# Two dense MLPs of a transformer kernel: the down product as seven block products instead of eight, with its block sums on GpSimd

## The reference, cut to what matters

```python
D_MODEL, SEQ, DEPTH, D_FF = 1024, 512, 2, 4096
...
def sqrelu_mlp(x, w_up, w_down):
    return jnp.square(jax.nn.relu(x @ w_up)) @ w_down
...
        x = layer_norm(ALPHA * x + mix, ln_gain[layer, 0], ln_bias[layer, 0])
        x = layer_norm(ALPHA * x + sqrelu_mlp(x, mlp_w_up[layer], mlp_w_down[layer]), ln_gain[layer, 1], ln_bias[layer, 1])
```

## Time and profile before

| what | value |
|---|---|
| median of three executions | 1917.28 us |
| their spread | 1913.70 to 1919.94 us |
| span of the profiled execution, first to last instruction | 1913.1 us |
| TensorE busy by the profile | 1859.2 us, 97% |
| VectorE busy | 1174.5 us, 61% |
| ScalarE busy | 773.4 us, 40% |
| GpSimd busy | 582.9 us, 30% |
| bytes read from HBM | 216.59 MB, 114 GB/s over the span |
| mean granted TensorE clock | 0.993 |

### The profile page before, as it was taken

How to read it: one execution, slowest core, us unless ns; L and a number is a source line. 1 busy time by engine, 2 the same in 40 slices (tenths; PEclk the granted TensorE clock), 3 DMA queues, 4 the chain that set the end, 5 groups by cost and what they waited for, 6 DMA issues and landing times.

```text
span 1913.1 us, 25510 instructions
## 1 busy us (share of the span) xinstructions
PE 1859.2 (97%) x9628; PEld 1519.7 (79%) x9628; DVE 1174.5 (61%) x2001; ACT 773.4 (40%) x1320; POOL 582.9 (30%) x442
## 2 busy tenths in 40 slices
PE   9999899999999999998999999999999999999997
PEld 7876568788888888866888888889887788888876
DVE  4568857742573542176775257555559788676766
ACT  4246643321332242385342133327445554434342
POOL 1234533100000010183210000115346557676740
PEclk9999999999999999999999999999999999999999
DMA  7321033643453132302255245421211323333344
GB/s 278 120 93 45 1 132 111 224 151 109 135 185 121 67 110 95 104 2 89 89 198 176 91 152 176 159 88 67 88 45 67 110 89 110 115 121 117 112 153 154
DMA packets 39392, 222.29 MB, mean 116 GB/s; under 512 B 5936, under 2 KB 6256, under 8 KB 18928
## 3 DMA queue, kind: packets, MB, share of 16 engines
q1 hardware_dynamic: 27616, 178.94, 26.2%
q0 software_dynamic: 11664, 41.80, 6.7%
HBM read 216.59 MB, written 2.10 MB: 114 GB/s over the span
## 4 chain that ended last, share of the span: by engine, by line
PE 78%; DVE 13%; DMA 3%; ACT 2%; POOL 2%; issue 2%; SPq 0%; POOLq 0%; ACTq 0%; DVEq 0%
PE G L421 35%; PE G L2674 7%; PE G L2560 5%; PE TR L2674 5%; PE OB L2674 5%; PE G L2581 4%; PE TR L421 2%; DMA KS_sb<-ada 2%; PE OB L421 2%; PE G L1717 2%; POOL weights_low L460 1%; PE TR L2560 1%; DVE weights_low L460 1%; PE OB L1717 1%; PE TR L1717 1%
## 5 line engine op out<-in xcount | busy, mean ns | idle before, releaser
L460 DVE TENSOR_TENSOR weights_low<-ring_sb,weights_high 128x1024 fp32r<-128x1024 f32 x206 | 255.8, 1246 | 377.4 <-ACT weights_high L454 377.3
L454 ACT ACTIVATE weights_high<-ring_sb 128x1024 fp32r<-128x1024 f32 (+1 forms) x308 | 316.2, 1032 | 398.6 <-PE OB L2674 131.3
L421 PE MATMUL G<-xt_high,weights_high 128*128 128x512 f32 (+1 forms) x1224 | 451.3, 369 | 2.3 <-issue 1.5
L421 PE MATMUL G<-xt_low,weights_high 128*128 128x512 f32 (+1 forms) x1224 | 449.0, 367 | 0.0
L421 PE MATMUL G<-xt_high,weights_low 128*128 128x512 f32 (+1 forms) x1224 | 448.9, 367 | 0.0
L460 POOL TENSOR_TENSOR weights_low<-ring_sb,weights_high 128x1024 fp32r<-128x1024 f32 (+2 forms) x102 | 245.5, 2418 | 306.7 <-ACT weights_high L454 306.7
L421 PEld LDWEIGHTS G<-xt_high,weights_high 128*128 128x128 f32 x1224 | 228.4, 187 | 43.1 <-issue 3.6
L421 PEld LDWEIGHTS G<-xt_high,weights_low 128*128 128x128 f32 x1224 | 228.4, 187 | 38.6
L421 PEld LDWEIGHTS G<-xt_low,weights_high 128*128 128x128 f32 x1224 | 228.4, 187 | 37.6
L2435 POOL DMA_DIRECT2D KS_sb<-ada x64 | 34.0, 531 | 472.2 <-DVE og_sb L3040 472.2
L2274 DVE SCALAR_TENSOR_TENSOR KS_sb<-G,cols_sb,KS_sb 128x441 f32<-128x441 f32 (+2 forms) x160 | 109.9, 687 | 65.1 <-ACT KS_sb L1991 65.1
(11 more groups left out here) (576 smaller groups left out, 3657.4 us busy)
## 6 DMA issues: line engine op xcount, KB each, us to landing
ring_sb<-chunks SPq DMA_DIRECT2D x155, 1024.0 KB, 4.9
KS_sb<-ada POOLq DMA_DIRECT2D x64, 512.0 KB, 4.7
wide_sb<-x_features SPq DMA_DIRECT2D x4, 512.0 KB, 9.2
X_sb<-slabs SPq DMA_DIRECT2D x1, 2048.0 KB, 13.9
ring_sb<-slabs SPq DMA_DIRECT2D x1, 2048.0 KB, 7.7
rows_sb<-ln_gain POOLq DMA_DIRECT2D x4, 512.0 KB, 5.1
rows_sb<-ln_bias POOLq DMA_DIRECT2D x4, 512.0 KB, 6.0
X_sb<-x SPq DMA_DIRECT2D x4, 512.0 KB, 8.8
```

The source lines that it names most:

```text
L421: mm = nc.tensor.matmul(out, lhsT=a, rhs=b, start=(3 * i + j == 0), stop=(3 * i + j == n - 1))
L454: nc.scalar.activation(quarter_part(weights(stage, n)[0], stage, n), quarter_part(raw_quarter(Q), stage, n), ACT.Copy).then_inc(w_hi, 1)
L460: tt_(out=quarter_part(wl, stage, n), in0=quarter_part(raw_quarter(Q), stage, n), in1=quarter_part(wh, stage, n), op=ALU.subtract).then_in ...
```

## The change

All 32 up quarters of an MLP now run first, and their squares stay in float32 in `wide`. The down product is then Strassen's algorithm in Winograd's order on 2x2 blocks: the 512 tokens in two halves (A1., A2.), the features in pairs of tiles (the two of a pair are the two block columns), the output in two halves of 512 columns. A pair of feature tiles is a unit; there are 16. For each unit seven block products are summed instead of eight, each 2 token tiles x 3 = 6 matmuls of 512 columns. PSUM holds only four such products at a time, so there are two sweeps over the units: P1, P2, P5, P3 first, then P6, P4, P7; the down weights are loaded twice. GpSimd makes the block sums in float32: four sums of 128x256 of the hidden features and one of 128x512 of the weights per unit in the first sweep, three of 128x512 of the weights in the second. ScalarE and VectorE then split the summed blocks into high and low parts: per unit two quarters of weights and two 128x512 blocks of features in the first sweep; 1024 and 512 columns of weights, 512 and 256 columns of features in the second. VectorE adds the finished products into `X` in 28 steps per MLP (16 before). The loads of gain and bias wait for the second sweep; the small inputs of the second block load during the first sweep of `mlp1`; the context's transposes are split in two.

```diff
-    st.add("mlp0", quarters=64, act=32, hidden=32, dve=16, ln=28, std=4)
+    st.add("mlp0", quarters=96, act=32, dve=28, ln=28, std=4)
...
+        def block_low(dve, stage, x, u):
+
+            dve.wait_ge(staged_h, staged_at(stage, x, u))
...
+            nc.vector.tensor_tensor(out=lo, in0=src, in1=hi, op=ALU.subtract).then_inc(staged_l, 1)
...
+            def last_units(stage):
+
+                q, w = st(stage, "quarters"), SPLIT0[stage] + SWEEP2
+                for u in range(2, UNITS):
+                    if u < 4:
+                        sp.wait_ge(quarters, q + SWEEP1 + 28)
+                    else:
+                        sp.wait_ge(w_lo, w + 2 * (u - 4) + 2)
+                    sp.dma_start(raw_unit(u), A["chunks"][w // 2 + u]).then_inc(raw_in[u % 2] if u % 4 < 2 else raw_x[u % 2], 16)
...
+                if NORMS[n] in MLPS:
+                    gp.wait_ge(quarters, st(NORMS[n], "quarters") + SWEEP2 + 6)
                 gp.dma_start(rows[:, 0, :], gain.partition_broadcast(P)).then_inc(gb_in, 16)
...
             gpsimd_low(gp, "mlp0")
-            gain_bias(1, A["ln_gain"][0, 1, :], A["ln_bias"][0, 1, :])
...
+                def first_weights(u):
+                    Q = SPLIT0[stage] + SWEEP1 + 2 * u
+                    gp.wait_ge(raw_in[(Q // 2) % 2], 16 * (Q // 4 + 1 - SPARED.get(stage, 0)))
+                    b11, b12 = raw_quarter(Q)[:, 0:512], raw_quarter(Q + 1)[:, 0:512]
+                    tt(out=b12, in0=b12, in1=b11, op=ALU.subtract).then_inc(raw_sums, 1)
...
+                    room_for(gp, stage, u)
+                    tt(out=s1, in0=a21, in1=a22, op=ALU.add).then_inc(hid_sums, 1)
+                    gp.wait_ge(staged_l, staged_at(stage, "0", u))
+                    gp.wait_ge(hid_sums, n + 1)
+                    tt(out=a21, in0=a11, in1=a21, op=ALU.subtract).then_inc(hid_sums, 1)
+                    gp.wait_ge(hid_sums, n + 2)
+                    tt(out=a11, in0=s1, in1=a11, op=ALU.subtract).then_inc(hid_sums, 1)
+                    gp.wait_ge(hid_sums, n + 3)
+                    tt(out=s4, in0=a12, in1=a11, op=ALU.subtract).then_inc(hid_sums, 1)
...
+                    unit_landed(gp, stage, u)
+                    tt(out=b12, in0=b22, in1=b12, op=ALU.subtract).then_inc(raw_sums, 1)
+                    gp.wait_ge(raw_sums, n + 1)
+                    tt(out=b11, in0=b12, in1=b11, op=ALU.add).then_inc(raw_sums, 1)
+                    gp.wait_ge(raw_sums, n + 2)
+                    tt(out=b21, in0=b11, in1=b21, op=ALU.subtract).then_inc(raw_sums, 1)
...
+                for u in range(1, UNITS):
+                    first_weights(u)
+                    hidden_sums(u)
+                    if stage == "mlp1" and u == 5:
+                        gpsimd_inputs(gp)
+                for u in range(UNITS):
+                    second_weights(u)
+                    if u == 6:
+                        gain()
...
+            def down_high(act, stage, n):
...
+                if n % 2:
+                    act.wait_ge(raw_sums, raw0 + (n - SWEEP1) // 2 + 1)
+                high_split(act, stage, n)
...
+                for u, ts in ((12, (0, 1)), (13, (0, 1)), (14, (0,)), (15, (0,)), (14, (1,)), (15, (1,))):
+                    second_ready("p6", u)
...
+                for u in (12, 15):
+                    for x in ("p4", "p7"):
...
+                tile0_turned(0)
+                for t in range(2):
+                    for u in (13, 14):
+                        for x in ("p4", "p7"):
...
+                        tile0_turned(1)
+                        tile1_turned()
```

More of the change, by code:

```diff
@@ L144, in build @@
     st.add("x_ctx", tr=4)
-    st.add("mlp1", quarters=64, act=32, hidden=32, dve=16, ln=52, std=8, norm=4)
+    st.add("mlp1", quarters=96, act=32, dve=28, ln=52, std=8, norm=4)
     st.add("x4", tr=8)
@@ L480, in n_quarters, with hid, hid_r, flat @@
         def n_quarters(stage):
-            return len(FFN) if stage == "ffn2" else sum(a + b for a, b in PARTS[stage])
+            return len(FFN)
+        def hid(c):
+            return wide[:, c, :]
+        def hid_r(c):
+            return (Hh, Hl)[c // 16][:, c % 16, :]
+        def flat(x):
+            return x.rearrange("p a b -> p (a b)")
+        def staged_rows(u, x):
+            if u == 0:
+                return rowsr[:, x, :], rowsr[:, 2 + x, :], flat(rows[:, :, :])[:, (2 + x) * S:(3 + x) * S]
+            r = 2 * (u % 4) + x
+            return XTh[:, r, :], XTl[:, r, :], ring[:, 0, r * S:(r + 1) * S]
@@ L2607, in ada_turn, with turn_context @@
                 nc.tensor.transpose(OB[0][:, P:2 * P], ogf[:, 0:P], ident).then_inc(ada_turned, 1)
[L2609 to L2613, removed]
+            def turn_context(r):
+                if r == 0:
+                    pe.wait_ge(ln_norm, st("ln_ctx", "norm") + 2)
+                    pe.wait_ge(dve_out, st("mlp1", "dve") + 16)
+                else:
+                    pe.wait_ge(tr_out, st("x_ctx", "tr") + 2)
+                for b in range(4 * r, 4 * r + 4):
@@ L3165, in layer_norm @@
                 started = LN_ORDER[stage][:TT] == EARLY
-                for op, t in LN_ORDER[stage][TT if started else 0:]:
+                for op, t in LN_ORDER[stage][TT if started else 2 if stage in MLPS else 0:]:
                     if (op, t) in hooks:
@@ L3345, in _ @@
             xt_low_tile("x1", 0, 3)
-            mlp("mlp0", ALPHA, 0, between("x2", 8, True))
+            mlp("mlp0", ALPHA, 0, lambda chain, last, low: {
+                ("ga", 0): low, ("bi", 0): lambda: chain(0), ("bi", 1): lambda: (chain(1), xt_low_tile("x2", 8, 0)), ("s0", 2): lambda: xt_low_tile("x2", 8, 1)})
             xt_low_tile("x2", 8, 2)
@@ L3368, in _ @@
             xt_low_tile("x3", 16, 3)
-            mlp("mlp1", ALPHA, 2)
+            mlp("mlp1", ALPHA, 2, lambda chain, last, low: {
+                ("ga", 0): low, ("bi", 0): lambda: chain(0), ("bi", 1): lambda: chain(1), ("s0'", 1): lambda: last(2)}, tile2_early=True)
             vector_second(dve, down_wait, layer_norm, first_half)
```

655 lines of the change are left out of this document (464 added, 191 removed), and 3 rows, old and new, of the table ADA_STEPS.

## The result

The changed kernel takes 2017.87 us (median of 4 runs, 2015.9 to 2021.19), the kernel before, on the same chip, 1915.49 us (1913.12 to 1919.94): a ratio of 1.0531, with a 95% interval of 1.0511 to 1.0551. The forecast was 2010 us, within 1932 to 2050. The profiled execution took 2019.65 us, 1.7 us more than its span. The forecast let the median stand 4.2 us above the span, as before; here the two are level (2017.87 and 2018.0). So the time rose by 102.4 us by the medians and by 104.9 us by the spans, where the forecast had 92.7.

What follows compares the result with a forecast made beforehand. The prediction took TensorE to bound the MLPs before the change, and GpSimd's and VectorE's common access to bound both sweeps after it. 1917.3 + 90 (both MLPs) + 3.7 (small loads) - 1 (`ada`) = 2010 us, range 1932 to 2050.

Steps and rivals of the forecast that it cites:

- The engines take turns: Down sweeps: GpSimd and VectorE, both reading two SBUF tensors, exclude each other and bound both sweeps; +45 us per MLP.
- The price of a turn: Down sweeps: VectorE's instructions add 2.83 and 2.08 us to GpSimd's time, making units 7.04 and 5.98 us.
- high bound: Down phases: hand-overs of 0.1 us per dependent GpSimd sum, 5 us at the change of sweeps; +61 per MLP, 2042.
- The tail: End of each down phase: the layer norm delays the last products, 17.9 us after the last low part, not 8.2.
- the gap named as a sign: End of each down phase: TensorE idles some 10 us between its last but one and last group.
- The seven loads: First sweep of `mlp1`: seven small loads in GpSimd's queue, 0.53 us each, add 3.7 us.
- The `ada` terms: Up phases: moved gain and bias loads relieve the first `ada` load, -1 us in `mlp0`; nothing in `mlp1`.
- Tiles 2 and 3: Behind each down phase: three additions where one stood delay their norms for the next stage, 2 us per MLP.
- the gain and bias loads: Second sweep, unit 6: their 1.1 us issue on GpSimd fits into the buffers' slack and costs nothing.
- Hidden: Both sweeps: loading weights a second time, 32 MB, costs nothing; a chunk lands in 4.9 us, within a unit.
- TensorE stays the bound: Rival, down sweeps: turns cost little, units 5.44 and 4.08 us; about 1900 us, 1877 with layer norm hidden; chance 0.11.
- The clock: Rival, down sweeps: TensorE's waits lower its clock to 1.2 GHz, units 9.7 and 7.3 us, about 2150 us; chance 0.03.

Runs made afterwards that it cites:

- run 1: Changed kernel with VectorE's low parts in the down phases made copies of the high parts, reading one SBUF tensor in place of two: 1916.02 us (one run).
- run 2: Changed kernel with GpSimd's sums of weight blocks cut to 8 columns in both sweeps, the hidden sums kept: 1922.23 us (one run).
- run 3: Changed kernel with all block sums of both MLPs moved from GpSimd into VectorE's queue, all computed: 1967.97 us, ratio 1.0277 to the kernel before.
- run 4: Changed kernel with the seven small loads of the second MLP's first sweep moved behind all its block sums: 2021.31 us, ratio 1.0553 to the kernel before.
- Run 9: Changed kernel with three of TensorE's `ada` sums per MLP one up product later, all computed: 2022.19 us, ratio 1.0566 to the kernel before.
- run 8: Changed kernel with the gain and bias loads issued behind GpSimd's last sums of the second sweep: 2020.65 us, ratio 1.0537 to the kernel before.
- run 6: Changed kernel with VectorE's eight additions from PSUM at the change of sweeps cut to 8 columns: 2018.32 us, ratio 1.0529 to the kernel before.

## Why the prediction was right, and where it was not

**The engines take turns: right.** Runs 1 to 3 each take one side's use of the common access away, and each time the units come down to what is left. With the turns gone no other bound stood in the way: a unit took TensorE's 5.44 us, and 4.1 to 4.4 in the second sweep. So in the sweeps the removed products are worth what the forecast said.

**The price of a turn: right within about 5%, and in the second sweep on the other engine.** First sweep: 6.89 us for 7.04. The five sums' means add up to 6.66 us, 2.45 more than alone, with 0.23 us of hand-overs that the forecast had only in its high bound. Second sweep: the forecast let GpSimd set the pace, 3.90 + 2.08. GpSimd took about 5 us per unit and waited for weights; VectorE, busy throughout, set it with 6.2 to 6.3 us. The error is small because the shared access is what counts, whichever engine is charged. Both are under the full sums of the two engines' times alone (8.05 and 6.9 us). So for the Trainium skill's statement that the blocked side waits for the whole instruction ("SBUF — State Buffer"; for two SBUF inputs it stands in the section "Summary: rules for kernel authors"), the trace agrees on the exclusion and not on that price as a sum: a first-sweep unit took 6.89 us for 8.05.

The forecast had 201.3 us from the end of the up products to the last low part ahead of the norm. In `mlp0` that is 497.2 to 697.5 us, 200.3: GpSimd's first sweep ends 3 us earlier than forecast, and the second sweep takes 2 us longer. With the tail's 2 us more, the down phase of `mlp0` comes out 0.1 us from its term (+43.4 for +43.3): that close it is by luck, since these errors cancel.

**The tail: 17.9 forecast, 19.9 measured** (697.5 to 717.4 us). Tile 1 was to be ready 14.3 us after that low part; it took 14.8. TensorE still had 54 products to do at that low part, not 36, so the gap named as a sign is 3.95 us and not some 10. Its end in the timeline after, which answers to the earlier trace rows:

```profile
708.72 1.28 DVE L3394 TENSOR_TENSOR xt_low<-TR,xt_high 128x512 fp32r<-128x512 f32 x2
708.85 2.35 POOL L489 TENSOR_TENSOR weights_low<-ring_sb,weights_high 128x1024 fp32r<-128x1024 f32 x1 [0.42 <-ACT weights_high L483]
709.92 2.37 DVE L3608 SCALAR_TENSOR_TENSOR X_sb<-X_sb,rstd_sb,rows_sb 128x1024 f32<-128x1024 f32 x1
...
712.38 0.45 PE L2722 MATMUL OB<-table_sb,X_sb 128*128 128x128 f32 x1 [3.95 <-issue]
```

VectorE's last scaling stands behind tile 0's low parts, as forecast, and takes 2.37 us in place of 1.28 beside GpSimd's low part for the next stage: a turn the forecast had left out. TensorE, after its wait, starts at the lower clock: the transposes take 1.60 us to the next product, where the first tile's took 0.80, and the six products behind them 2.06 us in place of 1.36. The wait put down to "issue" is the one for that scaling.

**The seven loads, +3.7 us: wrong** (run 4: nothing). The failed step is to have added an issue time on one engine to the sum while another engine was held up in the same place: the context's norm, which the kernel before had in its down run, hidden behind TensorE, and which the forecast did not price once that cover was gone. The norm's price is one of crowding too: in run 1, where VectorE has time to spare, norm and loads together lengthen their unit by 1.5 us. With the norm, `mlp1` came out at 45.9 us for 47.0 by luck.

**The `ada` terms, -1 us and nothing: wrong**, +3.2 and +3.4 us. The first load, on the chain before, has left it, with two others of the first up run; but four later ones have come onto it. The first of them in the chain of the up phase of `mlp0` (start, duration, what):

```profile
372.35 1.23 DVE weights_low L489
373.58 0.68 DVE og_sb L3373
374.38 0.49 issue
374.88 5.26 DMA KS_sb<-ada
380.17 0.76 DVE og_sb L3373
380.96 0.76 DVE og_sb L3373
381.77 0.43 PE OB L2825 x8
```

The load waits for VectorE's product of the piece before, which the new order puts behind a weight's low part, and TensorE's sum comes 8 us after that. The forecast priced the load that moved, not the order around the others. Run 9 shows that moving TensorE's sums doesn't help; another order on VectorE wasn't tried. The timelines point to a further cause: the last four sums of `mlp0` stood four up products apart before (513.4, 535.7, 558.1 and 580.4 us), without a wait, and stand three apart now (432.0, 449.9, 467.5, 485.8), 17.0 us of TensorE's work, while loads and products for one sum take 17.6 to 18.3 us. These waits grew by 2.2 us in `mlp0`; the other 1.0 us is not traced, and no run has the sums four apart.

**Tiles 2 and 3, +2 us: right in `mlp0`** (TensorE waits 2.5 us for tile 2 there), **too little in `mlp1`** (5.9 us in `w_in`). Its weights' high parts stand on ScalarE behind the norm's root, and TensorE waits for the low parts that GpSimd makes of them (timeline after):

```profile
1399.15 0.20 ACT L3090 ACTIVATE rstd_sb<-rstd_sb 128x1 f32<-128x1 f32 x1 [0.64 <-DVE rstd_sb L3592]
1399.26 2.94 ACT L483 ACTIVATE weights_high<-ring_sb 128x1024 fp32r<-128x1024 f32 x3
...
1400.38 5.74 POOL L489 TENSOR_TENSOR weights_low<-ring_sb,weights_high 128x1024 fp32r<-128x1024 f32 x2 [9.39 <-ACT weights_high L483]
...
1403.82 0.58 PE L448 MATMUL G<-hidden_low,weights_high 128*128 128x256 f32 x1 [5.16 <-POOL weights_low L489]
```

**Costed at nothing and borne out:** the gain and bias loads (run 8) and the additions at the change of sweeps (run 6). "Hidden" for the second pass of weights held in its effect only: GpSimd waited 10 us for them in `mlp0`, while VectorE had no idle time to lose.

**The rivals.** That TensorE stays the bound fell, but run 1, which fulfils its condition, shows that its price was wrong: 1916 us (one run), not 1877 or 1900. The gain of 43.5 us is there in the sweeps and is spent elsewhere: the last 72 products of a down phase take 31.4 and 26.5 us where 16.3 would do, 15.1 and 10.2 us more (the forecast had 9.7 there and 2 behind), and the up phases and `w_in` pay as in the changed kernel. Without the contention, by that one run, the change would still be worth about nothing. The clock did fall in places, where the forecast took 1.00 for the sweeps. Five stretches of `mlp0`'s down phase, 30.6 us in all, ran at the lower of the two levels, 1.2 GHz; two of them:

```profile
595.70:602.50 6.80, 5.75 (x14) 4.50 (x15) 4.71 (x4) 1.56 (x4) 6.51 (x5) 0.51 0.43 157
...
687.80:698.00 10.20, 6.78 (x17) 4.77 (x16) 9.97 (x13) 4.41 (x6) 4.75 (x8) 0.51 0.31 104
```

The first begins within TensorE's wait of 4.1 us at the change of sweeps, the second behind a wait of 2.7 us. While VectorE or GpSimd sets the pace, slower products are done in time in which TensorE would have waited (argued, not tested); in the tail the lower clock costs about 1.5 us, on the second tile's transposes and the products behind them.

## What to carry to other kernels

Before work is given to an idle GpSimd, look in the trace for stretches where it and VectorE both read two SBUF tensors, and price the two as one resource; if the work must be of that kind, VectorE alone was the cheaper place here (run 3), since it holds the access for about half the time. A saving on the engine that hides everything else has to be set against what it was hiding: by run 1, the ends of the down phases (25 us), the up phases (7) and the stages behind the MLPs (8) cost nearly as much as an eighth of the products gave back (43.5). An issue time on an off-path engine belongs in the sum only if nothing else is late at the same place.

## What the runs showed of the hardware that was not expected

In the first sweep of `mlp0` TensorE waited some 1.2 us in every unit of 6.89 us, and the granted clock stayed at 1.00. In the second, with a wait of 1.6 to 2.7 us in most units, it fell to 0.51 at three places in `mlp0` and stayed at 1.00 between them; the forecast, going by an attention stretch, expected no fall in either. VectorE's `tensor_scalar` that also writes a sum takes 1.22 us for 1024 columns, as long as the subtraction of two tensors it replaced, with 0.08 us more for reading the sum out, and leaves GpSimd's sums at 1.30 and 0.74 us.
